# The 64-row sample tile of the down products: high and low halves side by side in one stationary block

## What is computed

```python
h = rmsnorm(x, g_pre_ffn)
gu = h @ w_gu                                  # 1024 x 5632
gate, up = gu[..., :D_FF], gu[..., D_FF:]      # D_FF = 2816
f = (jax.nn.silu(gate) * up) @ w_down          # 2816 x 1024
x = x + rmsnorm(f, g_post_ffn)
```

## Time and profile before

| | |
|---|---|
| median of 3 runs | 1721.84 us (1719.69 to 1723.24) |
| the profiled execution, its own time | 1715.88 us |
| its span | 1714.3 us |
| mean granted clock of TensorE | 0.966 |
| PE busy | 1591.7 us (93%) |
| DVE, ACT, POOL busy | 609.6, 402.6, 384.0 us |
| instructions | 23386, PE matmuls 9406 |

### The profile page before, as it was taken

One profiled execution on the slowest core, in us unless ns is written; L12 is line 12 of the kernel. 1 busy time (PEld: TensorE's weight loads), 2 busy tenths in 40 slices (PEclk: granted clock), 3 DMA queues, 4 the chain that ended last, 5 costly groups with the idle time before them and its releaser, 6 DMA issues.

```text
span 1714.3 us, 23386 instructions
## 1 busy us (share of the span) xinstructions
PE 1591.7 (93%) x9406; PEld 1378.1 (80%) x9406; DVE 609.6 (36%) x976; ACT 402.6 (23%) x697; POOL 384.0 (22%) x437
## 2 busy tenths in 40 slices
PE   6999999988968886988999999999999999999995
PEld 5788888878735554766889999999999999999994
DVE  2233110106546662443552232323333232332355
ACT  4300121211124442442332211111111121111111
POOL 4244310012322223001554111111111111111111
PEclk9999999997779998998999999999999999999997
DMA  5323334129161108973425645535455353544436
GB/s 190 101 100 123 123 122 158 46 75 311 53 202 51 50 13 334 384 308 89 145 89 184 166 117 153 153 103 165 115 146 147 115 153 107 155 138 129 134 90 185
DMA packets 120272, 245.29 MB, mean 143 GB/s; under 512 B 20652, under 2 KB 82364, under 8 KB 115045
## 3 DMA queue, kind: packets, MB, share of 16 engines
q1 hardware_dynamic: 111400, 157.15, 28.8%
q0 software_dynamic: 6976, 71.32, 13.8%
q10 hardware_dynamic: 1824, 15.83, 2.2%
HBM read 214.08 MB, written 106.21 MB: 187 GB/s over the span
## 4 chain that ended last, share of the span: by engine, by line
PE 52%; DVE 1%; issue 0%; POOL 0%; ACT 0%; POOLq 0%; DVEq 0%
PE y_ps L2089 30%; PE x_ps L2100 8%; PE y_ps L1719 6%; PE m_ps L2100 4%; PE d_ps L2100 4%; PE x_ps L1766 0%; DVE acc L2023 0%; PE m_ps L1713 0%; DVE acc L2027 0%; DVE acc L2014 0%; POOL stat L1913 0%; DVE m_lo L1665 0%; ACT m_hi L1626 0%; POOL f L1886 0%; DVE silu L2006 0%
## 5 line engine op out<-in xcount | busy, mean ns | idle before, releaser
L2089 PE MATMUL y_ps<-h_hi,gu_hi 128*128 128x384 f32 (+1 forms) x1056 | 345.9, 328 | 0.0
L2089 PE MATMUL y_ps<-h_hi,gu_lo 128*128 128x384 f32 (+1 forms) x1056 | 345.5, 327 | 0.0
L2089 PE MATMUL y_ps<-h_lo,gu_hi 128*128 128x384 f32 (+1 forms) x1056 | 345.4, 327 | 0.0
L1886 POOL TENSOR_TENSOR f<-silu,f 128x384 fp32r<-128x384 f32 (+1 forms) x66 | 63.5, 962 | 615.3 <-ACT f L1942 615.3
L2089 PEld LDWEIGHTS y_ps<-h_lo,gu_hi 128*128 128x128 f32 x1056 | 198.3, 188 | 1.9
L2089 PEld LDWEIGHTS y_ps<-h_hi,gu_hi 128*128 128x128 f32 x1056 | 198.2, 188 | 1.9
L471 PE MATMUL z_ps<-w_hi,h_hi 128*128 128x512 f32 x496 | 194.5, 392 | 5.4 <-POOL h_lo L327 5.4
L2089 PEld LDWEIGHTS y_ps<-h_hi,gu_lo 128*128 128x128 f32 x1056 | 198.2, 188 | 0.0
L471 PE MATMUL z_ps<-w_hi,h_lo 128*128 128x512 f32 x496 | 193.6, 390 | 0.0
L471 PE MATMUL z_ps<-w_lo,h_hi 128*128 128x512 f32 x496 | 193.6, 390 | 0.0
L2006 DVE TENSOR_TENSOR silu<-silu,y_ps 128x384 f32<-128x384 f32 (+1 forms) x66 | 35.1, 531 | 369.1 <-ACT silu L1940 363.6
(11 more groups left out here) (215 smaller groups left out, 2183.0 us busy)
## 6 DMA issues: line engine op xcount, KB each, us to landing
ks_sample<-cache_k_win POOLq DMA_DIRECT2D x60, 544.0 KB, 5.9
vs_sample<-cache_v_win POOLq DMA_DIRECT2D x60, 544.0 KB, 7.4
raw<-w_gu SPq DMA_DIRECT2D x84, 256.0 KB, 6.9
K<-cache_k_win SPq DMA_DIRECT2D x8, 2048.0 KB
w_raw<-w_in SPq DMA_DIRECT2D x14, 1024.0 KB
z_scratch<-z_out SPq DMA_DIRECT2D x56, 256.0 KB, 2.0
raw<-w_down SPq DMA_DIRECT2D x22, 512.0 KB, 4.9
zr<-z_scratch SPq DMA_DIRECT2D x8, 1024.0 KB, 10.3
```

What stands on the lines that cost most here:

```text
L1886: pool.tensor_tensor(f_lo[cut], f_t[:, 0:n], f_hi[cut].bitcast(F32), ALU.subtract).then_inc(f_lo_ready, 1)
L2089: mm = pe.matmul(bank[u % 2][:, 0:n], w[s][:, k, h, :], x[:, k, c:c + n], start=(k, m) == (0, 0), stop=(k, m) == (KT - 1, 2))
```

## The change

- ACT writes the high part of the 64 sample tokens not into `f_hi` but into columns 0 to 63 of a block of its own, `f_s`; POOL writes their low part into columns 64 to 127. A unit of the third chunk has now two copies on ACT (256 and 64 columns) and two subtractions on POOL instead of one each; the semaphore is raised by the second.
- For the sample tile, a half-tile of `down` has 2 terms per sub-block: `f_s` by the high weights and `f_s` by the low weights, 4 matmuls in place of 6. Partitions 0 to 63 of the result belong to the high part of f, 64 to 127 to the low part. DVE adds all 128 partitions to `acc`.
- At the end the two halves of `acc` are added by two plain float32 matmuls of 512 columns on PE with a 128 x 64 matrix `fold` (two identities), which DVE makes once. The result `folded` lies in PSUM, and ACT's square and DVE's scale read it there.
- The order of tiles in the last group is now 0, 1, 2, 3, 4, 5, sample, 6, 7 (`LAST_TILES`), for every queue. The fold stands on PE between the products of tile 6 and those of tile 7. The last load of the residual and the last store of y have 512 KB now, and were 256 KB.

```diff
+    LAST_TILES = (0, 1, 2, 3, 4, 5, PT, 6, 7)
...
+        f_s = at("f_s", [128, 2, SUB, 128], Layout.STAT + 160, F32R)
+        fold, folded = at("fold", [128, NS], Layout.SILU), out.y_ps[1][NS:128, :]
...
# POOL
-                    pool.tensor_tensor(f_lo[cut], f_t[:, 0:n], f_hi[cut].bitcast(F32), ALU.subtract).then_inc(f_lo_ready, 1)
+                    low = pool.tensor_tensor(f_lo[cut], f_t[:, 0:n_p], f_hi[cut].bitcast(F32), ALU.subtract)
+                    if n_p < n:
+                        low = pool.tensor_tensor(f_s[:, par, sub, NS:128], f_t[:, n_p:n], f_s[:, par, sub, 0:NS].bitcast(F32),
+                                                 ALU.subtract)
+                    low.then_inc(f_lo_ready, 1)
...
# ACT
-                    act.copy(f_hi[:, par, sub, c:c + n], f_t[:, 0:n]).then_inc(f_hi_ready, 1)
+                    n_p = prompt(c, n)
+                    high = act.copy(f_hi[:, par, sub, c:c + n_p], f_t[:, 0:n_p])
+                    if n_p < n:
+                        high = act.copy(f_s[:, par, sub, 0:NS], f_t[:, n_p:n])
+                    high.then_inc(f_hi_ready, 1)
...
+                def square(i):
+                    t = LAST_TILES[i]
+                    if t == PT:
+                        act.wait_ge(fold_done, 1)
+                    else:
+                        act.wait_ge(added, whole(i))
...
+                    src = folded if t == PT else acc[:, t, :]
...
# DVE
-                        dve.tensor_tensor(acc[cut], acc[cut], d_ps[(2 * (1 - par) + j) % 4][lo:128, :], ALU.add).then_inc(added, 1)
+                        dve.tensor_tensor(acc[cut], acc[cut], d_ps[(2 * (1 - par) + j) % 4], ALU.add).then_inc(added, 1)
...
+                        if u == UNITS - 1:
+                            dve.wait_ge(f_ready, UNITS * GROUPS)
+                            dve.tensor_tensor(fold[:, :], ident[:, 0:NS], ident[:, NS:128], ALU.add).then_inc(fold_ready, 1)
...
# PE
+                        hi, lo = (x[:, 1 - par, :, t * 128:t * 128 + 128] for x in (f_hi, f_lo)) if t < PT else (f_s[:, 1 - par], None)
+                        terms = ((hi, wd_hi), (hi, wd_lo), (lo, wd_hi)) if t < PT else ((hi, wd_hi), (hi, wd_lo))
...
+                        if u < UNITS - 1:
+                            down(GROUPS, 1, 6 * (u - 3), 6)
+                down(GROUPS, 1, 12, 4)
+                pe.wait_ge(fold_ready, 1)
+                pe.wait_ge(f_ready, UNITS * GROUPS)
+                pe.wait_ge(added, whole(6))
+                for c in (0, 512):
+                    mm = pe.matmul(folded[:, c:c + 512], fold[:, :], acc[:, PT, c:c + 512], start=True, stop=True)
+                mm.then_inc(fold_done, 1)
+                down(GROUPS, 1, 16, 2)
```

More of the change, by code:

```diff
@@ L1786, in out_and_ffn @@
     rows = lambda t: slice(128 - tile_rows(t), 128)
-    whole = lambda t: 4 + GROUP_D * (GROUPS - 1) + 2 * t + 2
+    whole = lambda i: 4 + GROUP_D * (GROUPS - 1) + 2 * i + 2
+    LAST_TILES = (0, 1, 2, 3, 4, 5, PT, 6, 7)
     with ExitStack() as ctx:
@@ L1812, in out_and_ffn @@
                            "down_done", "added", "zeroed"))
+        fold_ready, fold_done = sem("fold_ready"), sem("fold_done")
+        prompt = lambda c, n: min(n, SEQ - c)
         piece = lambda g, e, p: 6 * g + 2 * e + p
@@ L1850, in step, with load_x @@
                         load_gu(g, 2, 2 * g + 2)
-                def load_x(t):
-                    sp.dma_start(x_m[t % 2][rows(t), :],
-                                 x_mid[t * 128:t * 128 + tile_rows(t), :]).then_inc(x_landed[t % 2], 16)
+                def load_x(i):
+                    t = LAST_TILES[i]
+                    sp.dma_start(x_m[i % 2][rows(t), :],
+                                 x_mid[t * 128:t * 128 + tile_rows(t), :]).then_inc(x_landed[i % 2], 16)
                 out.sync(sp, lambda eng: load_gu(0, 0, 0, first_gu))
@@ L1867, in _ @@
                 load_x(1)
[L1868 to L1871, removed]
+                for i, t in enumerate(LAST_TILES):
+                    sp.wait_ge(y_ready, i + 1)
+                    if i + 2 < TT:
+                        load_x(i + 2)
                     to = (A["y_prompt"][0, t * 128:t * 128 + 128, :] if t < PT
@@ L1909, in _, with root @@
                 pool.wait_ge(half_set, 2)
-                def root(t):
-                    pool.wait_ge(mean_ready, t + 1)
+                def root(i):
+                    t = LAST_TILES[i]
+                    pool.wait_ge(mean_ready, i + 1)
                     pool.tensor_tensor(stat[:, 2, t:t + 1], stat[:, 1, t:t + 1], mhalf[:, :], ALU.pow).then_inc(rstd_ready, 1)
@@ L1960, in step @@
                     unit(g, par, 5)
[L1962 to L1965, removed]
+                def square(i):
+                    t = LAST_TILES[i]
+                    if t == PT:
+                        act.wait_ge(fold_done, 1)
+                    else:
+                        act.wait_ge(added, whole(i))
+                    if i:
+                        act.wait_ge(squared, i)
                     else:
                         act.wait_ge(lo_ready, piece(LAST, 2, 2))
-                    act.activation(squares[rows(t), :], acc[rows(t), t, :], ACT.Square,
-                                   accum_out=stat[rows(t), 0, t:t + 1]).then_inc(squared, 1)
+                    src = folded if t == PT else acc[:, t, :]
+                    act.activation(squares[rows(t), :], src, ACT.Square, accum_out=stat[rows(t), 0, t:t + 1]).then_inc(squared, 1)
                 out.scalar(act, lambda eng, p: split((p,), first_gu, gu(0), 32))
@@ L2010, in add, with mean, scale @@
                     for j in range(first, first + count):
-                        lo = 64 if j // 2 == PT else 0
-                        cut = (slice(lo, 128), j // 2, slice(j % 2 * 512, j % 2 * 512 + 512))
+                        t = LAST_TILES[j // 2] if known(g, GROUPS) else j // 2
+                        cut = (slice(None), t, slice(j % 2 * 512, j % 2 * 512 + 512))
                         dve.wait_ge(down_done, GROUP_D * g + j + 1)
-                        dve.tensor_tensor(acc[cut], acc[cut], d_ps[(2 * (1 - par) + j) % 4][lo:128, :], ALU.add).then_inc(added, 1)
-                def mean(t):
-                    dve.wait_ge(squared, t + 1)
+                        dve.tensor_tensor(acc[cut], acc[cut], d_ps[(2 * (1 - par) + j) % 4], ALU.add).then_inc(added, 1)
+                def mean(i):
+                    t = LAST_TILES[i]
+                    dve.wait_ge(squared, i + 1)
                     dve.tensor_scalar(stat[rows(t), 1, t:t + 1], stat[rows(t), 0, t:t + 1], 1.0 / D_MODEL, EPS,
                                       ALU.mult, ALU.add).then_inc(mean_ready, 1)
-                def scale(t):
-                    dve.wait_ge(rstd_ready, t + 1)
-                    dve.scalar_tensor_tensor(acc[rows(t), t, :], acc[rows(t), t, :], stat[rows(t), 2, t:t + 1],
+                def scale(i):
+                    t = LAST_TILES[i]
+                    src = folded if t == PT else acc[:, t, :]
+                    dve.wait_ge(rstd_ready, i + 1)
+                    dve.scalar_tensor_tensor(acc[rows(t), t, :], src, stat[rows(t), 2, t:t + 1],
                                              g_post[rows(t), :], ALU.mult, ALU.mult).then_inc(scaled, 1)
-                    dve.wait_ge(scaled, t + 1)
-                    dve.wait_ge(x_landed[t % 2], 16 * (t // 2) + 16)
-                    dve.tensor_tensor(acc[rows(t), t, :], acc[rows(t), t, :], x_m[t % 2][rows(t), :],
+                    dve.wait_ge(scaled, i + 1)
+                    dve.wait_ge(x_landed[i % 2], 16 * (i // 2) + 16)
+                    dve.tensor_tensor(acc[rows(t), t, :], acc[rows(t), t, :], x_m[i % 2][rows(t), :],
                                       ALU.add).then_inc(y_ready, 1)
@@ L2095, in down @@
                     for j in range(first, first + count):
-                        end, col = min(j // 2 * 128 + 128, NTOK), j % 2 * 512
+                        t = LAST_TILES[j // 2] if known(g, GROUPS) else j // 2
+                        col = j % 2 * 512
                         pe.wait_ge(added, GROUP_D * (g - 1) + j + 1)
+                        hi, lo = (x[:, 1 - par, :, t * 128:t * 128 + 128] for x in (f_hi, f_lo)) if t < PT else (f_s[:, 1 - par], None)
+                        terms = ((hi, wd_hi), (hi, wd_lo), (lo, wd_hi)) if t < PT else ((hi, wd_hi), (hi, wd_lo))
                         for s in range(SUB):
-                            for m, (x, w) in enumerate(((f_hi, wd_hi), (f_hi, wd_lo), (f_lo, wd_hi))):
-                                mm = pe.matmul(d_ps[(2 * (1 - par) + j) % 4][:, :], x[:, 1 - par, s, end - 128:end],
-                                               w[:, s, col:col + 512], start=(s, m) == (0, 0), stop=(s, m) == (SUB - 1, 2))
+                            for m, (x, w) in enumerate(terms):
+                                mm = pe.matmul(d_ps[(2 * (1 - par) + j) % 4][:, :], x[:, s, :], w[:, s, col:col + 512],
```

(4 more changed lines are left out.)

3 lines of the change are left out of this document (2 added, 1 removed).

## The result

The changed kernel took 1709.66 us (median of 5 runs, 1707.67 to 1713.05) against 1721.84 us (5 runs, 1718.16 to 1723.44): ratio 0.9939, 95% interval 0.9924 to 0.9954. That is 10.5 us less by the ratio, and the median lies 1.8 us under the range that was forecast. Compared twice more, the same two kernels gave 0.9961 (0.9947 to 0.9974) and 0.9956 (0.9943 to 0.9970). Without the first five executions of the changed kernel it would be 6.5. The forecast was 7.3.

A forecast was written before the change was run, and what follows sets the result against it. PE, busy without a gap at 2.4 GHz, was taken to bound the groups, and a DVE, POOL, DVE chain the end. Terms -9.07 + 0.36 + 1.40 = -7.3 us gave 1714.5 us, 8-in-10 range 1711.5 to 1718.5.

The forecast's parts named there:

- The groups: Ten feed-forward groups ahead of the last part: four sample-tile matmuls fewer each, 0.907 us a group, 9.07 us less.
- The first rival: In the groups, removed matmuls give back only their weight load, 172 ns each: 6.9 us, sum -5.1 us; chance 0.06.
- the 131 ns of the Trainium skill: In the groups, the skill page's matmul spacing in place of 227 ns: 5.2 us for ten groups, sum -3.5 us.
- the slower case of `f_s`: In the groups, two matmuls in a row on one `f_s` block are dearer; up to +10.8 us; chance 0.05.
- The wait for the last low part: Ahead of the last part, PE waits longer for split ACT copy and POOL subtraction: +0.36 us, bounds nothing to +1.0.
- The last part: After the groups, the first mean waits for fold and sample square, starting at 9.20 instead of 7.80: +1.40 us.
- The rival of a clock that stays down through the fold: In the last part, half clock lasts through the fold: up to +4.8 us over the term; chance 0.14.
- The end: At the block's end, doubled last store and residual load cost nothing; POOL's drain moves with its last power instruction.
- the rival that it hides the tail: At the end, POOL's drain counts from its last window copies, so wait and fold terms vanish: -9.1 us; chance 0.09.
- The sum: Whole kernel: -9.07 + 0.36 + 1.40 = -7.3 us, giving 1714.5 us, 0.42% less.
- the difference is carried over: The profiled execution lay 6.0 us under the runs' median, so -7.3 us was applied to that median, 1721.84 us.
- the drain rival: At the end, POOL's drain counts from its window copies and hides the tail: 1712.8 us; chance 0.09.

The follow-up runs named there:

- two_terms: The kernel before, with only the sample tile's third term (low part of f by the high weights) left out; 1710.79 us, ratio to before 0.9943.
- six_terms: The changed kernel with a third term for the sample tile again (high-by-low matmul once more); 1723.96 us, ratio to before 1.0025.
- before_again: The kernel before, unchanged, timed once more against itself; 1720.49 us, ratio 1.0000.
- sample_last: The changed kernel with the fold behind all down products and the tiles in order 0 to 7, sample; 1714.54 us, ratio to before 0.9955.
- root_act2: The changed kernel with tile order 6, sample, 7, fold behind all down products, both last tiles' powers moved from POOL to ACT and DVE; 1706.17 us, ratio to before 0.9923.

## Why the prediction was right or wrong

**The groups** were forecast at 9.07 us and gave 8.5. The price of a removed matmul was right: two_terms, which removes them and nothing else, gives 0.90 us a group, 9.0 us. What the prediction put at nothing is the `f_s` block, 0.05 us a group beside two_terms and 0.09 beside before in six_terms, some 0.5 us in ten groups; a half-tile of four takes 0.93 us with it and 0.91 without. Why is not shown. All cover that the prediction named held, since PE shows no idle time in 571 us. The first rival, matmuls worth only a weight load (6.9 us), and the 131 ns of the Trainium skill (TensorE: Matmul & The Clock Gate, Back-to-back issue gap; 5.2 us) are excluded by the groups of two_terms. So is the slower case of `f_s`.

**The wait for the last low part** was to grow by 0.36 us. From ACT's Silu to PE's first matmul it grew from 3.82 us (1683.34 to 1687.16) to 4.32 (1673.11 to 1677.43). Half of it is not the split: copy and subtraction together went from 1.45 to 1.69 us, +0.24, and DVE's product stood 0.25 us later behind a residual load that had landed late. Without any split the same stretch is 4.17 us in before_again and 4.33 in two_terms. So the term is 0.24 us for the 0.36 forecast.

**The last part** was to lose 1.40 us through the fold. In the two profiled executions it lost 1.5 (19.3 to 20.8), the fold took 1.93 us for the 1.89 forecast, and the mean is at 9.57 for 9.20. The chain mean, scale, add behind it was kept, as the prediction had it. Over two and three traces the difference is 1.0 (20.0 to 21.0), since the half-clock phase in before differs by 2.9 us from one execution to the other. The rival of a clock that stays down through the fold was not seen in any trace of the changed kernel; its price was, in sample_last.

**The end.** The doubled store was hidden behind POOL's drain, as forecast, and the drain follows the last power instruction: the rival that it hides the tail is out.

**The sum** of 7.3 us was right within what can be measured: 7.3 by the traces behind the block ahead, 7.5 by all executions (6.5 without the first five). That it agrees to a tenth is luck: the terms as measured, 8.5 less 0.2 to 0.5 for the wait less 1.0 to 1.5 for the fold, give 6.5 to 7.3.

**The step that failed** is the one from the sum to the range, "1711.5, the drain rival less a spread of 1.3 us of a median", and under it "the difference is carried over" to a median of 3 runs. Two things in it were mis-sized. The base of 1721.84 us lies 1.3 us over the mean of all 57 executions of before. And single executions of either kernel scatter by 2.4 to 2.6 us; from that I estimate 1.25 x 2.6 / sqrt(5) = 1.5 us for a median of five and 1.25 x 2.4 / sqrt(3) = 1.7 for the base of three, 2.3 us together where the range had 1.3. The measured median is 4.8 us under the forecast, about twice that.

In the traces most of the scatter lies in the stages ahead, which with identical instructions take 393.7 to 403.5 us, longer where PE is granted 1.2 GHz for longer; behind them the traces of the changed kernel differ by 1.2 us and those of before by 2.0. I had one trace of before, and did not ask what its unchanged stages would do next time, though it lay 6 us under the median of the runs beside it; that was the sign.

The scatter does not explain all of it. The five executions of the first comparison had a mean of 1710.2 where the fourteen of the two later ones had 1714.0, and of all ways to pick five from these nineteen only about 1 in 400 sets them as far apart. Only one of the five was traced; its stages ahead were the shortest of all 13 traces. Whether the chip or the time of the first comparison made its five low stays open, as does why the phases at half clock fall differently from one execution to the next.

## What to carry to other kernels

Where an engine is busy without a gap, a removed matmul gave back its spacing here, and two experiments that remove or restore it alone settle that at once. Put a helper step (here the fold) behind the work that someone waits for, and look which engine's list is queued behind it. Look also at which engine's drain ends last: the two moved power instructions were worth more than half of what the removed matmuls gave. When one profiled execution lies far from the timed ones, compare the stages that no edit touches before the range is drawn; and compare kernels from a mark behind those stages.

## What the runs showed of the hardware

- POOL's drain at the end of a block in which it had issued 124 DMAs takes 10.636 to 10.647 us in twelve traces, and 0.85 us with 4 DMAs; all of them had landed before it began. It is on the path when POOL has a late instruction: moving two of 0.55 us to other engines brought the end from 7.9 us behind the last add to 3.1.
- The same 992 matmuls of the prompt attention took 157.9 us at a mean granted clock of 0.97 and 161.0 us at 0.96, in two executions of one program.
- The fold, two plain float32 matmuls of 512 columns that are four instructions in the trace, took 1.93 us at full clock and 3.65 us at half clock.
- In root_act2 ACT squared two tiles after a square root without loading a table again; the one load took 1.28 us.
